# A two-block transformer kernel: coupling matrices carried across partition halves by products with the identity, and a late norm factor in the last feed-forwards

## What is computed

```python
m = jnp.where(strict, jnp.einsum('bhncd,bhnsd->bhncs', kb, kc) * decay, 0.0)
tmat = lax.linalg.triangular_solve(m + eye, eye, left_side=True, lower=True, unit_diagonal=True)
```

```python
m = rmsnorm(h, norm_mlp_pre[i])          # y * rsqrt(mean(y*y) + eps) * g
m = jnp.square(jax.nn.relu(jnp.einsum('bsd,df->bsf', m, w_up[i])))
m = jnp.einsum('bsf,fd->bsd', m, w_down[i])
h = h + rmsnorm(m, norm_mlp_post[i])
```

## Time and profile before

| | |
|---|---|
| median of 3 runs | 2202.15 us (2195.95 to 2207.38) |
| the profiled execution's own time | 2200.06 us |
| its span in the trace | 2198.2 us |
| TensorE (PE) busy | 2125.0 us, 97% |
| DVE, ACT, POOL busy | 56%, 23%, 6% |
| mean granted TensorE clock | 0.99 of full |
| HBM read | 286.15 MB, 131 GB/s |
| chain that ended last | PE 87%, DVE 6%, ACT 3%, DMA 2%, issue 1% |

### The profile page before, as it was taken

One profiled execution on the slowest core, in us unless ns is written; L12 is line 12 of the kernel. 1 busy time (PEld: TensorE's weight loads), 2 busy tenths in 40 slices (PEclk: granted clock), 3 DMA queues, 4 the chain that ended last, 5 costly groups with the idle time before them and its releaser, 6 DMA issues.

```text
span 2198.2 us, 34562 instructions
## 1 busy us (share of the span) xinstructions
PE 2125.0 (97%) x14676; PEld 1514.4 (69%) x14676; DVE 1230.1 (56%) x2175; ACT 504.0 (23%) x1038; POOL 135.5 (6%) x148
## 2 busy tenths in 40 slices
PE   7999888999999999999999999999999999999998
PEld 4446666554788885457466995686895488779646
DVE  2664444477745456652356775485666428666643
ACT  2434323352300000022162100223210022411101
POOL 0003323000000000003100000002000000200000
PEclk9999999999999999999999999999999999999999
DMA  8122344404422223446203444333344443334441
GB/s 352 58 77 80 125 179 161 164 20 176 169 77 96 77 96 134 172 153 134 77 2 115 167 163 175 139 117 120 131 170 172 155 151 115 116 125 165 172 177 71
DMA packets 42952, 291.00 MB, mean 132 GB/s; under 512 B 5296, under 2 KB 7728, under 8 KB 8496
## 3 DMA queue, kind: packets, MB, share of 16 engines
q1 hardware_dynamic: 39344, 279.99, 35.0%
q0 software_dynamic: 1312, 3.15, 1.1%
q10 hardware_dynamic: 2144, 5.65, 0.7%
HBM read 286.15 MB, written 1.05 MB: 131 GB/s over the span
## 4 chain that ended last, share of the span: by engine, by line
PE 87%; DVE 6%; ACT 3%; DMA 2%; issue 1%; ACTq 0%; POOL 0%; DVEq 0%
PE banks L1036 22%; PE banks L1564 16%; PE banks L1753 12%; PE banks L2935 6%; PE banks L2276 6%; PE banks L417 5%; PE banks L1957 2%; PE banks L816 1%; PE banks L2929 1%; DMA arena<-mix 1%; PE banks L455 1%; PE banks L644 1%; PE banks L831 1%; PE banks L852 1%; PE banks L822 1%
## 5 line engine op out<-in xcount | busy, mean ns | idle before, releaser
L1036 PE MATMUL banks<-arena 128*128 128x512 f32 x392 | 186.2, 593 | 0.7 <-DVE arena L1809 0.5
L1036 PE MATMUL banks<-weight_ring,arena 128*128 128x512 f32 x338 | 156.8, 593 | 0.0
L1036 PEld LDWEIGHTS banks<-arena 128*128 128x128 f32 x392 | 74.1, 190 | 93.7 <-issue 92.3
L1564 PE MATMUL banks<-normed,weight_ring 128*128 128x128 f32 x1040 | 130.9, 283 | 2.5 <-DVE normed L561 1.3
L2935 PE MATMUL banks<-normed,weight_ring 128*128 128x256 f32 x576 | 130.9, 388 | 1.2 <-DVE normed L561 0.6
L1564 PEld LDWEIGHTS banks<-normed,weight_ring 128*128 128x128 f32 x1040 | 125.8, 198 | 3.8 <-issue 3.2
L2276 PE MATMUL banks<-normed,weight_ring 128*128 128x512 f32 x288 | 126.1, 593 | 0.0
L2935 PEld LDWEIGHTS banks<-normed,weight_ring 128*128 128x128 f32 x576 | 110.9, 194 | 18.8 <-issue 2.5
L1001 DVE TENSOR_TENSOR arena<-weight_ring 128x512 f32<-128x512 f32 x67 | 46.2, 690 | 136.8 <-PE banks L1036 136.7
L1036 PEld LDWEIGHTS banks<-weight_ring,arena 128*128 128x128 f32 x338 | 63.5, 190 | 76.5 <-issue 75.7
L1564 PE MATMUL banks<-normed,arena 128*128 128x128 f32 x960 | 116.0, 275 | 0.0
(11 more groups left out here) (485 smaller groups left out, 3845.5 us busy)
## 6 DMA issues: line engine op xcount, KB each, us to landing
weight_ring<-in_weights SPq DMA_DIRECT2D x266, 1024.0 KB, 4.8
residual<-in_tokens ACTq DMA_DIRECT2D x1, 2048.0 KB, 15.0
mix<-in_rpb POOLq DMA_DIRECT2D x32, 64.0 KB, 3.6
constants<-in_const ACTq DMA_DIRECT2D x1, 1953.5 KB, 11.1
arena<-mix ACTq DMA_DIRECT2D x16, 64.0 KB, 8.3
out<-residual SPq DMA_DIRECT2D x1, 1024.0 KB, 4.8
branch<-arena POOLq DMA_DIRECT2D x1, 512.0 KB, 5.1
normed<-in_ple POOLq DMA_DIRECT2D x1, 512.0 KB, 3.7
```

The costliest lines, as they stand in the source:

```text
L1036: return pe.matmul(self.bank[i], left, b, start=(p == 0), stop=(p == n - 1))
L1564: mm = pe.matmul(o, a[:, k * P:k * P + P], right[:, k], start=(k == 0), stop=(k == H - 1))
```

## The change

In the delta stage the four DMAs of a pair are removed. PE carries the halves by products with a block of the identity into 256 columns of bank 2u + 1, and ACT copies them to C (`g_brought`); C now holds in its first four places what stays and in its last four what was brought, and the products L1944 index L accordingly. PE's `move(j + 1)` stands between `scan(j)` and `outputs(j)`, for the first pair between the gate projection and `across(0, 0)`; `across` of level 0 waits for `g_brought`, since it writes the same bank.

In `squared_pairs` the norm before the up projection goes. A new class `LateFactor` has ACT write gain times residual (without the factor) straight to u; the squares are taken after that by ACT, added up by DVE (`presum`, after add_weights(1)), summed over partitions by PE (`sums`, within `products` before the last product of pair 1), and the inverse root is spread by PE (`spread`, after product 1 of pair 2). ACT keeps it in SBUF, and POOL multiplies the quarters z of each group by it before ACT's relu: two instructions of 128x512 for each of the eight groups.

```diff
     def products(self, pe, k_ready, sums=None, spread=None, kept=()):
...
         for i in (7, 5, 6):
             self.product(pe, 1, i)
+        if sums:
+            sums(pe)
         self.product(pe, 1, 4).then_inc(self.sg["f_products"].sem, 1)
         for p in range(2, self.n):
...
-            for i in (1, 2, 4, 7, 5, 6):
+            self.product(pe, p, 1)
+            if p == 2 and spread:
+                spread(pe)
+            self.product(pe, p, 4)
+            if p == 2:
+                need(pe, kept)
+            for i in (2, 7, 5, 6):
                 self.product(pe, p, i)
+class LateFactor:
...
+    def scale(self, act):
+        lat = slice(S, T2)
+        for k in range(KT):
+            need(act, self.src_ready(k))
+            act.activation(self.out[:, k], self.h[:, k, lat], ACT.Copy, scale=self.gain(k, 1)).then_inc(self.sg["n_gained"].sem, 1)
+        for k in range(KT):
+            if k >= 4:
+                need(act, [self.hit("n_presummed", max(1, k - 4))])
+            act.activation(self.square[:, k % 4], self.h[:, k, lat], ACT.Square).then_inc(self.sg["squared"].sem, 1)
+
+    def presum(self, dve):
+        for k in range(1, KT):
+            need(dve, [self.hit("squared", k + 1)])
...
+            dve.tensor_tensor(out=self.total, in0=first, in1=self.square[:, k % 4], op=ALU.add).then_inc(self.sg["n_presummed"].sem, 1)
+
+    def sums(self, pe):
+        need(pe, [self.hit("n_presummed", KT - 1)])
+        for t in range(S // P):
+            mm = pe.matmul(self.K.psum[:, 1, t:t + 1], self.total[:, t * P:t * P + P], self.K.c("ones")[:, 0:1], start=True, stop=True)
...
+    def spread(self, pe):
+        need(pe, [self.hit("row_inverses", 1)])
+        for t in range(S // P):
+            mm = pe.transpose(self.K.bank(1)[:, t * P:t * P + P], self.K.token_inverse[:, t:t + 1].to_broadcast([P, P]), self.K.c("ident"))
...
+def squared_pairs(K, made, hidden, token_sums, y, late):
...
+    def gpsimd(pool):
+        need(pool, late.kept())
+        factor = bc(late.factor.rearrange("p (t n) -> p t n", t=2), 1, 2)
+        for g in range(n):
+            need(pool, [made.hit("f_quarters", g + 1)])
+            for x in range(2):
+                z = made.z[:, 0:4, x * P:x * P + P].rearrange("p (f t) n -> p f t n", t=2)
+                ins = pool.tensor_tensor(out=z, in0=z, in1=factor, op=ALU.mult)
+            ins.then_inc(scaled.sem, 1)
     def scalar(act):
+        late.scale(act)
+        late.root(act)
+        late.keep(act)
         for g in range(n):
             made.take_first(act, g)
-            need(act, [made.hit("f_quarters", g + 1)])
+            act.wait_ge(scaled.sem, sc + g + 1)
...
     def vector(dve):
         made.add_tokens(dve, k_ready)
         made.add_weights(dve, 1)
+        late.presum(dve)
         for g in range(n):
             for p in (2 * g + 2, 2 * g + 3):
                 if p < made.n:
                     made.add_weights(dve, p)
+                if p == 2:
+                    late.invert(dve)
@@ delta_stage, tensor
+        def move(j):
+            for u in range(2):
+                pe.wait_ge(sg["g_c"].sem, at["g_c"] + per["g_c"] * j + u + 1)
+                for p in range(2):
+                    other = L[u][1][halves[1 - p], 4 * p:4 * p + 4, :].rearrange("p i n -> p (i n)")
+                    mm = pe.matmul(K.psum[halves[p], 2 * u + 1, 0:256], K.c("ident")[halves[1 - p], halves[1 - p]], other, start=True, stop=True)
+                mm.then_inc(sg["g_moved"].sem, 1)
...
         last_gate["product"](pe)
+        move(0)
         across(0, 0)
...
             scan(j)
+            if j + 1 < NP:
+                move(j + 1)
             outputs(j)
@@ delta_stage, scalar
                 act.wait_ge(sg["g_c"].sem, at["g_c"] + per["g_c"] * j + u + 1)
                 for p in range(2):
-                    act.dma_start(C[u][halves[p], 4 - 4 * p:8 - 4 * p, :], L[u][1][halves[1 - p], 4 * p:4 * p + 4, :]).then_inc(moved[u].sem, 16)
+                    act.activation(C[u][halves[p], 0:4, :], L[u][1][halves[p], 4 * p:4 * p + 4, :], ACT.Copy)
             for u in range(2):
-                for p in range(2):
-                    ins = act.activation(C[u][halves[p], 4 * p:4 * p + 4, :], L[u][1][halves[p], 4 * p:4 * p + 4, :], ACT.Copy)
-                ins.then_inc(sg["g_stayed"].sem, 1)
+                act.wait_ge(sg["g_moved"].sem, at["g_moved"] + per["g_moved"] * j + u + 1)
+                act.activation(C[u][:, 4:8, :], K.bank(2 * u + 1, 256).rearrange("p (i n) -> p i n", i=4), ACT.Copy).then_inc(sg["g_brought"].sem, 1)
@@ delta_stage, gpsimd, level 1
-                        pool.wait_ge(moved[u].sem, mv[u] + 32 * (j + 1))
-                        pool.wait_ge(sg["g_stayed"].sem, at["g_stayed"] + per["g_stayed"] * j + u + 1)
+                        pool.wait_ge(sg["g_brought"].sem, at["g_brought"] + per["g_brought"] * j + u + 1)
@@ program
-            kr, _ = modulated_norm(K, h, S, S, plain("norm_mlp_pre"), None, u2, [], tiles, spread_bank=1)
-            down, r = squared_pairs(K, pairs, hidden, down_sums, token_y, kr)
+            down, r = squared_pairs(K, pairs, hidden, down_sums, token_y, LateFactor(K, h, plain("norm_mlp_pre"), u2, tiles))
```

More of the change, by code:

```diff
@@ L1565, in product, with products @@
         return mm
-    def products(self, pe, k_ready):
+    def products(self, pe, k_ready, sums=None, spread=None, kept=()):
         self.product(pe, 0, 1, k_ready)
@@ L1642, in gated_pairs, with __init__, hit, gained @@
     return down, made.banks_free()
[L1645 removed]
+class LateFactor:
+    def __init__(self, K, h, gain, out, src_ready):
+        self.K, self.h, self.gain, self.out, self.src_ready = K, h, gain, out, src_ready
+        counts = {"n_gained": KT, "squared": KT, "n_presummed": KT - 1, "summed": 1, "rooted": 1, "row_inverses": 1, "spread_inverses": 1, "n_factor": 1}
+        self.sg = {c: K.counter(c) for c in counts}
+        self.at = {c: self.sg[c].reserve(x) for c, x in counts.items()}
+        self.square = K.square.rearrange("p i (j n) -> p (i j) n", n=S)
+        self.total, self.factor = K.root[:, 0, 0:S], K.root[:, 0, S:2 * S]
+    def hit(self, name, i):
+        return (self.sg[name], self.at[name] + i)
+    def gained(self, k):
+        return [self.hit("n_gained", k + 1)]
+    def scale(self, act):
[10 more added lines that the diff above has]
+            need(dve, [self.hit("squared", k + 1)])
+            if k > 1:
+                need(dve, [self.hit("n_presummed", k - 1)])
+            first = self.square[:, 0] if k == 1 else self.total
+            dve.tensor_tensor(out=self.total, in0=first, in1=self.square[:, k % 4], op=ALU.add).then_inc(self.sg["n_presummed"].sem, 1)
[3 more added lines that the diff above has]
+            mm = pe.matmul(self.K.psum[:, 1, t:t + 1], self.total[:, t * P:t * P + P], self.K.c("ones")[:, 0:1], start=True, stop=True)
+        mm.then_inc(self.sg["summed"].sem, 1)
+    def root(self, act):
+        need(act, [self.hit("summed", 1)])
+        act.activation(self.K.token_root[:, 0:2], self.K.psum[:, 1, 0:2], ACT.Sqrt, bias=self.K.c("eps"), scale=1.0 / D).then_inc(self.sg["rooted"].sem, 1)
+    def invert(self, dve):
+        need(dve, [self.hit("rooted", 1)])
+        dve.reciprocal(self.K.token_inverse[:, 0:2], self.K.token_root[:, 0:2]).then_inc(self.sg["row_inverses"].sem, 1)
+    def spread(self, pe):
+        need(pe, [self.hit("row_inverses", 1)])
+        for t in range(S // P):
+            mm = pe.transpose(self.K.bank(1)[:, t * P:t * P + P], self.K.token_inverse[:, t:t + 1].to_broadcast([P, P]), self.K.c("ident"))
+        mm.then_inc(self.sg["spread_inverses"].sem, 1)
+    def keep(self, act):
+        need(act, [self.hit("spread_inverses", 1)])
+        act.activation(self.factor, self.K.bank(1, S), ACT.Copy).then_inc(self.sg["n_factor"].sem, 1)
+    def kept(self):
+        return [self.hit("n_factor", 1)]
@@ L1675, in vector @@
         down.add_tokens(dve, 3)
-    K.add(tensor=lambda pe: made.products(pe, k_ready), scalar=scalar, vector=vector)
+    K.add(tensor=lambda pe: made.products(pe, k_ready, late.sums, late.spread, late.kept()), scalar=scalar, vector=vector, gpsimd=gpsimd)
     return down, made.banks_free()
```

12 lines of the change are left out of this document (7 added, 5 removed).

## The result

The changed kernel takes 2178.93 us (median of 4 runs, 2177.52 to 2185.7). The kernel before took 2200.49 us beside it (4 runs, 2195.95 to 2207.38). The ratio is 0.991, with a 95% interval of 0.9891 to 0.9929. The forecast was 2178.0. Its profiled execution took 2177.56 us with a span of 2175.7 us, 22.5 us under the span of before.

The account below looks back on a forecast made before the run. PE, busy 97% of the span, was taken as the bound, so gains come from its standstills and lower clock. 14.5 us (delta stage) plus 9.4 (feed-forwards) made 23.9 off 2200.06, 2176.2; with 2.1 for the median, 2178, range 2166 to 2193.

Parts of the forecast that it names:

- Passages: Delta stage, three pair-to-pair passages: removing the transfers frees 17.65 us, less 2.4 us of costs, giving 15.2 us (12.0 to 17.65).
- The Trainium skill's fixed cost: Passages: at about 2.0 us per DMA, removing transfers would give nothing and cost 2.4 us; set aside for traced 9.4 to 9.9.
- First pair: Delta stage, first pair: `move(0)` and ACT's copy delay it 1.3 us, half charged, 0.7 us lost (0 to 1.3).
- Stage: Whole delta stage, the three passages less the first pair's loss: 14.5 us gained.
- no fall of the clock there: Sign of being right: PE's granted clock does not fall at the three passages, where it was 0.50 of full.
- Last feed-forwards: Start of each of the last two feed-forwards: 5.8 us earlier less 1.1 us inserted, 4.7 us each, 9.4 together.
- the first rival: Only the delta stage pays, the feed-forward gain eaten by DVE's additions, PE stops and a fallen clock: 2187.6 us, chance 12%.
- It started at 1568.53 before: 5.8 us: Last feed-forward: product (1,3) would start at 1562.7 instead of 1568.53, 5.8 us earlier.
- the low bound: Last feed-forwards, 2 us a layer: the clock falls once after the new starts and stops (1.7 us), presum 1 us late.
- POOL's price: Last feed-forwards: POOL's products by the norm factor take 1.1 us each, 2.2 us a group.
- The cover: Last feed-forwards: POOL's products cost PE nothing, DVE needing at most 8.3 us, or 10.5 with POOL, of 12.8 a group.
- The slower rival: Last feed-forwards: POOL becomes the bound from 2.25 us a product on; 2234 us at 4 us a product, chance 3%.

Follow-up runs that it names:

- before_again: The kernel before, unchanged, run and profiled a second time; 2202.98 us, one run.
- pad_first: The kernel before with eight unread PE products of 256 columns ahead of the first pair's first `across`, transfers kept; 2199.87 us, one run.
- order_alone: The kernel before with only the product order from pair 2 on changed to 1, 4, 2, 7, 5, 6, 3 in two-operand feed-forwards; 2200.83 us, ratio 1.0003.
- ff_only: The kernel before with only the last two feed-forwards' part of the change, coupling still by transfers; 2191.66 us, ratio 0.9965.
- factor_tripled: The changed kernel with four more chained POOL products of 128x512 in each group of the last feed-forwards; 2224.01 us, ratio 1.0123.
- delta_only: The kernel before with only the delta stage's part, identity products in place of transfers, feed-forwards as before; 2184.07 us, ratio 0.9925.
- hold_chunks: The kernel before with transfers kept, SP holding back three weight chunks per passage until the next pair's transfers land; 2186.29 us, ratio 0.995.

## Why the prediction was right, and where it was not

- **Passages: right in sum; one term right by luck.** I predicted 15.2 us. From the fill to the end of the level they give 4.93, 4.65 and 5.27, together 14.85. Over all traces the three passages take 49.9 to 52.1 us in five of the old code and 34.6 to 36.3 in six of the new with single products, 15.3 us less by the means. PE is the last to arrive, as said. `move` is 1.08 us of work (1.05 predicted), but it delays the outputs by 0.1 us and not by the 0.8 that I took for each passage. What ate the rest is the first level: I gave it 3.49 us, and over the new traces it takes 4.4 on average, because of stalls named issue of up to 2.0 us that I had not taken in. The two misses cancel. ACT's extra copies cost nothing.
- **The Trainium skill's fixed cost: rightly set aside, for a reason now shown.** The row of 9.4 to 9.9 us decided, but I didn't say what it was made of. 2.0 us are the transfer by itself, and the rest came with the weight chunks. Had I looked at the DMA share beside it, 0.97 from 240 to 250 us against 0.40 from 189 to 200 where the first pair's transfers took 2.0 us, I could have named the other remedy.
- **First pair: right in mechanism, and not to be seen in the profiled pair.** I charged 0.7 us, between 0 and 1.3, as half of a delay that the stall may take in. Both cases occur: without the stall the new code is 1.2 us later, and where the stall is there it ends at the same time as in the old code and takes the delay in. Which of the two an execution will have was not to be forecast.
- **Stage: right, to within its scatter.** 14.5 predicted. Five traces of the old stage (before, before_again, pad_first, order_alone, ff_only) come to layer 0's long product at 582.4 to 587.5, mean 585.1. Six of the new one with single products come at 570.6 to 574.6, mean 571.6: 13.5 us, with a scatter of 5 us in the old and 4 in the new. In the old stage the clock falls in four to six places, three of them behind the passages; in the new one once, in `factor_tripled` twice. I had said "no fall of the clock there", and that is so at every passage of the profiled execution.
- **Last feed-forwards: mechanism right; what the gain is made of was not said.** The (1,3) product was due 11.4 us after the residual and came at 11.24. PE's stops at pair 0 and pair 1 are 0.49 and 0.57 us, for DVE as predicted, half as long as the 1 us that the first rival gives them, and the clock stays full through them. The term "It started at 1568.53 before: 5.8 us" holds a fallen clock of 1.6 us, which the old start has in some kernels and not in others; in `order_alone` it is 1568.40 - 1552.74 = 15.66, so 4.4 us, and after the inserted products 3.3 remain of the 4.7. I had the window at clock 0.50 and used it only for the low bound. Against the kernel before, which has the fall in both its traces, 4.8 were measured for 4.7. That the new start is without the fall was not argued.
- **POOL's price: wrong by half, harmless.** 1.59 us a product instead of 1.1, and a DVE addition beside it 0.97 on average instead of 0.68 (1.64 for additions that lie wholly beside POOL's products in `factor_tripled`). The cover was there, as predicted.
- **The slower rival: right sort, wrong ring.** It asked for DVE's 8.3 us plus POOL's to pass 12.8, from 2.25 us a product on. What binds first is the ring ACT, DVE, POOL, with 8.5 us. 4 us are free, so by this sum two products could grow to about 3.5 us each before it closes, an estimate that no run tests; the DVE delays of `factor_tripled` would bring it down. The Trainium skill ("SBUF — State Buffer", Who interferes with whom) has a DVE instruction with two SBUF inputs and a GpSimd one that reads SBUF exclude each other. The rows agree: an addition of 0.69 us and a product of 1.05 to 1.1 take 1.64 to 1.67 each when they overlap, close to their sum. Both get longer, and in the changed kernel both have the time to spare.
- **Terms that weren't there, and luck in the sum.** The layer-1 stretch gave 1.6: the old trace has a fall of the clock there, the new one has none, and `order_alone` shows nothing by the median for the one line that changed in it. The attention between the feed-forwards took 2.9 more: it has 1.7 us of falls in the old trace and 4.6 in the new, in unedited code. The predicted terms measured 14.1 + 9.6 = 23.7 in this pair, and these two bring it to 22.5. Without any clock fall in the feed-forwards the change is worth 13.5 to 14.1 for the stage and 6.6, together 20.1 to 20.7 us. The three comparisons of the changed kernel with before give medians 21.6, 20.5 and 22.1 us apart. The forecast of 2178.0 for 2178.93 is closer than such sums can be, and part of that closeness is luck.

What stays open: what makes the stalls named issue and the clock falls keep or change their place. I have no run that moves one at will, and why the profiled executions are mostly faster than their kernels' medians was not looked into.

## What to carry to other kernels

When a small transfer on the critical path takes many times its own cost, look at what else is in the DMA queues at that moment: holding bulk loads back for it was worth as much here as moving the data by other means. Read the price of an inserted piece at the place itself, over several traces, and not at the end of a stage that scatters by more than the price. Before charging a saved stretch to an edit, check the granted clock in both halves of the comparison, and read the same instructions in a second trace. For a new stage on an idle engine, trace the ring through all the queues that it joins, not only the engine's own load.

## What was not expected of the hardware

- A clock fall can recur at one place (102.32, 102.36 and 102.36 us for the same 896 instructions in three traces of the old start) and be absent there (100.73 in `order_alone`, `delta_only` and `hold_chunks`) in kernels that differ elsewhere. One such fall costs 1.6 us where PE is full.
- In the stage of short products (64x64) the chain's pieces named issue of over 0.25 us add up to 5 to 13 us in every kernel, the longest stall on PE 2.56 us. Their places differ between kernels, and between executions of one.
- Carrying 256 columns from one partition half to the other by the identity takes PE 1.08 us for four halves, nearly all of it hidden here, and ACT 0.81 for the two copies. The four DMAs for the same took 2.0 us alone and 8.5 behind weight chunks.
